# Down blocks of the experts with two neighbouring rows on each partition, and transposes that read every second column

## What is computed

```python
def swiglu(x, w_gate, w_up, w_down):
    return (jax.nn.silu(x @ w_gate) * (x @ w_up)) @ w_down

def moe_swiglu(x, w_router, w_gate, w_up, w_down):
    ...
    for e in range(N_EXPERTS):
        out = out + combine[..., e:e + 1].astype(x.dtype) * swiglu(x, w_gate[e], w_up[e], w_down[e])
    return out
```

## Time and profile before

| | |
|---|---|
| median of 3 runs | 1136.45 us (1135.53 to 1136.66) |
| the profiled execution, its own time | 1137.84 us |
| its span, first to last instruction | 1136.0 us |
| TensorE busy | 1107.8 us (98%), 5842 matmuls |
| VectorE, ScalarE busy | 643.2 us (57%), 467.8 us (41%) |
| moved by DMA | 300.08 MB, mean 264 GB/s |
| chain that ended last | PE 87%, DMA 5%, DVE 3%, ACT 2%, issue 2% |

### The profile page before, as it was taken

One profiled execution on the slowest core, in us unless ns is written; L12 is line 12 of the kernel. 1 busy time (PEld: TensorE's weight loads), 2 busy tenths in 40 slices (PEclk: granted clock), 3 DMA queues, 4 the chain that ended last, 5 costly groups with the idle time before them and its releaser, 6 DMA issues.

```text
span 1136.0 us, 14603 instructions
## 1 busy us (share of the span) xinstructions
PE 1107.8 (98%) x5842; PEld 813.6 (72%) x5842; DVE 643.2 (57%) x745; ACT 467.8 (41%) x598; POOL 43.8 (4%) x45
## 2 busy tenths in 40 slices
PE   7999999999999999999999999999999999999996
PEld 6777878888887788876666666666666666666664
DVE  4877675545467886764655534554553465555235
ACT  4556544443335565143344433333343343443220
POOL 3000020000014000000000000000000000000001
PEclk9999999999999999999999999999999999999998
DMA  9943266555546600089999999899999989999962
GB/s 297 345 147 115 86 196 201 185 185 185 171 163 207 228 1 1 1 295 386 357 367 353 350 353 385 293 394 377 326 388 362 376 295 382 375 350 378 359 270 78
DMA packets 126814, 300.08 MB, mean 264 GB/s; under 512 B 4970, under 2 KB 7160, under 8 KB 126736
## 3 DMA queue, kind: packets, MB, share of 16 engines
q1 hardware_dynamic: 124336, 291.52, 71.2%
q0 software_dynamic: 2112, 6.87, 2.2%
q10 hardware_dynamic: 288, 0.63, 0.2%
HBM read 297.88 MB, written 1.12 MB: 263 GB/s over the span
## 4 chain that ended last, share of the span: by engine, by line
PE 87%; DMA 5%; DVE 3%; ACT 2%; issue 2%; SPq 0%; POOL 0%; POOLq 0%; DVEq 0%; ACTq 0%
PE bank L1599 23%; PE bank L1600 21%; PE bank L1671 12%; PE bank L2064 7%; PE bank L1699 6%; PE bank L2074 4%; PE bank L1789 2%; PE bank L1898 2%; DMA raw<-in_w_in 2%; DMA raw<-in_moe_w_gate 1%; PE bank L1883 1%; PE bank L1815 1%; PE bank L2042 1%; PE bank L1604 1%; DMA raw<-in_moe_w_up 1%
## 5 line engine op out<-in xcount | busy, mean ns | idle before, releaser
L1439 DVE TENSOR_TENSOR w_lo<-raw,w_hi 128x2048 fp32r<-128x2048 f32 x83 | 190.3, 2292 | 271.6 <-ACT w_hi L909 271.6
L1599 PE MATMUL bank<-w_hi,xT_hi 128*128 128x512 f32 (+1 forms) x784 | 312.1, 400 | 0.5 <-ACT w_hi L737 0.5
L1600 PE MATMUL bank<-w_hi,xT_lo 128*128 128x512 f32 (+1 forms) x784 | 302.6, 388 | 0.0
L909 ACT ACTIVATE w_hi<-raw 128x2048 fp32r<-128x2048 f32 x83 | 158.7, 1912 | 240.0 <-PE bank L1671 133.4
L1032 DVE TENSOR_TENSOR w_lo<-raw,w_hi 128x2048 fp32r<-128x2048 f32 x62 | 142.0, 2291 | 103.5 <-ACT w_hi L728 103.0
L1599 PEld LDWEIGHTS bank<-w_hi,xT_hi 128*128 128x128 f32 x784 | 147.9, 189 | 64.4 <-issue 25.6
L1600 PEld LDWEIGHTS bank<-w_hi,xT_lo 128*128 128x128 f32 x784 | 148.1, 189 | 27.2
L1671 PE MATMUL bank<-w_lo,xT_hi 128*128 128x512 f32 (+1 forms) x640 | 167.4, 384 | 0.1
L728 ACT ACTIVATE w_hi<-raw 128x2048 fp32r<-128x2048 f32 x64 | 122.6, 1918 | 97.6 <-PE bank L1671 45.0
L1671 PEld LDWEIGHTS bank<-w_lo,xT_hi 128*128 128x128 f32 x640 | 118.2, 188 | 24.5 <-DVE w_lo L1042 0.5
L1599 PE MATMUL bank<-w_hi,hT_hi 128*128 128x512 f32 x312 | 124.7, 400 | 2.3 <-issue 2.3
(11 more groups left out here) (217 smaller groups left out, 1060.3 us busy)
## 6 DMA issues: line engine op xcount, KB each, us to landing
raw<-in_moe_w_up SPq DMA_DIRECT2D x70, 1024.0 KB, 9.0
raw<-in_moe_w_down SPq DMA_DIRECT2D x70, 1024.0 KB, 8.4
raw<-in_moe_w_gate SPq DMA_DIRECT2D x69, 1024.0 KB, 8.6
raw<-in_w_in SPq DMA_DIRECT2D x23, 1024.0 KB, 8.6
raw<-in_ffn_w_gate SPq DMA_DIRECT2D x11, 1024.0 KB, 5.1
raw<-in_ffn_w_up SPq DMA_DIRECT2D x11, 1024.0 KB, 5.2
raw<-in_ffn_w_down SPq DMA_DIRECT2D x11, 1024.0 KB, 4.9
raw<-in_w_out SPq DMA_DIRECT2D x8, 1024.0 KB, 6.1
```

The lines of the kernel that those rows point to most:

```text
L909: nc.scalar.activation(w_hi[:, m % NH, :], raw[:, n % NR, :], ACT.Copy).then_inc(hi_done, 1)
L1439: nc.vector.tensor_tensor(w_lo[:, m % NH, :], raw[:, (BASE_MOE + load[at[o]]) % NR, :], w_hi[:, m % NH, :].bitcast(F32), ALU.subtract).the ...
L1599: nc.tensor.matmul(o, hi, wh, start=start, stop=False)
L1600: nc.tensor.matmul(o, lo, wh, start=False, stop=False)
```

## The change

A down block puts rows 2p and 2p + 1 on partition p, which are neighbours in memory, 8 KB in all. Part k of the buffer now holds rows 2p + k. For the products to pair the same features, the transposes of the activations take for tile 2i + k not 128 columns in a row but every second of the 256 columns of block i, from column k on. Gate and up blocks, and the dense layer, stay as they are.

```diff
+        def hidden_rows(k, at=0):
+
+            first = at + k // 2 * 2 * P + k % 2
+            return slice(first, first + 2 * P - 1, 2)
+
...
                 if kind == "down":
-                    src = moe_w_down[0, bass.ds(e, 1), c * 256:(c + 1) * 256, :]
+                    src = moe_w_down[0, bass.ds(e, 1), c * 256:(c + 1) * 256, :].rearrange("o (p k) n -> p (o k) n", k=2)
                 else:
                     w = moe_w_gate if kind == "gate" else moe_w_up
                     k = D // 2
                     src = w[0, bass.ds(e, 1), part * k:(part + 1) * k, c * CW:(c + 1) * CW]
-                load(n, src.rearrange("o (k p) n -> p (o k) n", p=P), free, first)
+                    src = src.rearrange("o (k p) n -> p (o k) n", p=P)
+                load(n, src, free, first)
...
                 for k in range(4):
-                    ins = nc.tensor.transpose(bank[:, 4, k * P:(k + 1) * P], hid[:, tt, k * P:(k + 1) * P], ident)
+                    ins = nc.tensor.transpose(bank[:, 4, k * P:(k + 1) * P], hid[:, tt, hidden_rows(k)], ident)
...
                     ins = nc.tensor.transpose(bank[:, 5, k * SMALL:(k + 1) * SMALL],
-                                              hid_s[0:SMALL, c % 2, k * P:(k + 1) * P], ident[0:SMALL, 0:SMALL])
+                                              hid_s[0:SMALL, c % 2, hidden_rows(k)], ident[0:SMALL, 0:SMALL])
```

## The result

The changed kernel took 1142.21 us in the median of 5 runs (1141.12 to 1143.80), the kernel before 1136.45 (1134.61 to 1138.64): the ratio is 1.0057, 95% interval 1.0043 to 1.0071. The medians are 5.8 us apart, two and a half times the 2.3 us that the prediction took as what can be told from no change. The ratio is not the quotient of the two medians: times 1136 us it is 6.5 us, with an interval of 4.9 to 8.1.

The account below looks back on a forecast made before the run. The prediction took TensorE to bound the kernel. From the runs' median of 1136.45 us it took a 0.5 us gain from transfers and price 0 for transposes: 1135.9 us, range 1134.4 to 1140.4.

Parts of the forecast that it names:

- The bound: Expert stage: TensorE bounds it, busy 624.51 of 628 us; DMA has 70 us to spare over the stage.
- The transfers: Down-block loads: 8 KB pieces save 0.075 us a block, 5.3 us of DMA time over 70 blocks.
- What of it reaches the end: TensorE's 1.1 us wait for a gate block at 788.6 us: 0.5 us comes off, bounds 0 and 1.1.
- SyncE's queue: Down-load issue on SyncE: one DMA instruction a block before and after, 373 ns median; piece count hardly shows.
- The transposes: Expert activation transposes on TensorE: stepped weight loads stay at 139 and 137 ns, price taken as 0.
- The other value it had priced: Transposes' loads at the slow kind's pace: 4.3 us for small experts, 0.2 for large, together 4.5 us.
- The rule it leaned on: Transposes' stepped SBUF reads: step two of a 4-byte type has two hits a line, so price 0.
- The weight loads slow down: Rival at the 21 small-expert transpose groups: price 4.5 us, time 1140.4; chance 0.23.
- its far end: Rival for all 196 transposes: loads take twice 139 ns with no cover, 27 us, time 1163; chance 0.03.
- the pieces did not stay at 4 KB: Rival on down loads: the view's loops do not fold, pieces stay 4 KB, time 1136.4; chance 0.07.
- were not slower: Rival on down loads: longer pieces fall back to 2.70 us a block, time 1137.5; chance 0.04.
- lateness did not go for good: Rival on TensorE's waits for landings after 633 us: all 3.4 us removed, time 1133.0; chance 0.07.

Follow-up runs that it names:

- experiment 1: Against the kernel before: transposes step by two columns, down blocks loaded as before (wrong features, only time read); 1141.84 us, ratio 1.0053.
- experiment 2: Against the kernel before: down blocks in 8 KB pieces, transposes read neighbouring columns (wrong features, only time read); 1135.64 us, ratio 1.0002.
- experiment 8: The changed kernel once more, against the kernel before on the same chip; 1140.96 us, ratio 1.0045.
- experiment 5: Against the kernel before: only the 84 small-expert transposes step by two columns, down blocks as before (only time read); 1140.44 us, ratio 1.0040.
- experiment 4: Against the kernel before: 8 KB pieces, ScalarE and VectorE put even and odd columns apart so transposes read neighbours; 1136.77 us, ratio 1.0012.
- experiment 9: 8 KB pieces with columns put apart by ScalarE and VectorE ahead of the transposes, once more, against the kernel before; 1135.76 us, ratio 0.9996.

## Why the prediction was wrong, point by point

The forecast was 1135.9 us, a gain of 0.5; the measured time is 1142.2, above the range, and the direction is the one given 0.23.

- **The bound.** Right, but for one reading: the DMA row has 6 and 2 in its last two slices, not eight or nine in all but the last. TensorE's stream sets the time; experiment 1 puts 6.0 us on it with no change of a transfer, experiment 2 takes 8960 packets away with no change of the time.
- **The transfers.** The mechanism and its size were right: the views fold to pieces of 8 KB, 115376 packets as named, landings 2.45 us apart for 2.475 forecast (2.50 in experiment 2), and 5.7 us less queue time for 5.3. The page's estimate (the Trainium skill, DMA: Bandwidth & Descriptors, "Why small descriptors are slow (HBM only)") of 1.2% for this step was too small beside these 0.08 us of 2.55, some 3%; the trace's own step from 2 KB to 4 KB was the better guide.
- **What of it reaches the end.** The step named one wait of 1.1 us at 788 us and took half of it as the gain. In the first profile of the changed kernel the expert matmuls never wait for a landing. But in the profile of experiment 1, with its old 4 KB pieces, they don't either; in the second profile of the changed kernel (experiment 8) they wait as in the kernel before, and in that of experiment 5, with 4 KB pieces, more. Experiment 8 first, then 5:

```profile
PE bank L2070 <- DMA raw<-in_moe_w_gate: 1.2, 1, 1.2
PE bank L2070 <- DMA raw<-in_moe_w_up: 0.5, 1, 0.5
...
PE bank L2070 <- DMA raw<-in_moe_w_gate: 2.0, 2, 1.6
PE bank L2070 <- DMA raw<-in_moe_w_up: 0.5, 1, 0.5
PE bank L2080 <- DMA raw<-in_moe_w_down: 0.2, 1, 0.2
```

  Such waits come and go between executions of one kernel by a microsecond or two. The one in the profile can't be counted on in another execution, and reading a gain from it was a mistake, though a small one. Experiments 2, 4 and 9 put the pieces at 0.2 us slower, 1.4 us slower and 0.5 us faster, each with 1.2 to 1.4 us on either side, so a gain of 0.5 is neither shown nor excluded.
- **SyncE's queue.** That the count of pieces hardly shows in the instruction's time was read from two and four pieces a partition (373 ns for both). With one it takes 333 ns; nothing hung on it.
- **The transposes.** Here the prediction failed, at "I take 0, the row of the same instruction". A row with neighbouring columns says nothing of a stepped read, so a price of nothing had no row behind it, and the row of the slow kind (191 ns) turned out the nearer one: the stepped load takes 202 to 206. The other value it had priced was good: 0.204 us for a small group, measured 0.23; 4.3 us for the 21 groups, 4.8 by the rows and 4.5 in experiment 5. The large groups were put at 0.2 us and are 1.1 by the rows, where the matmuls now start (0.63 - 0.279) / 3 = 0.117 us apart for 0.109, about the pace of the stepped loads in a small group; in the time it is not to be told from none.
- **The rule it leaned on.** The Trainium skill (SBUF — State Buffer, the note on "cachelines") says that two hits on a line of 16 bytes keep the full rate. The trace disagrees: at two hits the bare transposing loads go from 0.061 us apart to (0.55 - 0.206) / 3 = 0.115, and at one hit they take hardly longer (207 ns for 206). It stood in the prediction as an aside, but beside the unstepped row it is the only thing there that speaks for a price of 0.
- **The rivals.** "The weight loads slow down" is what happened, with its place and size: 1140.4 forecast, 1142.2 and, in the second comparison, 5.1 us over its own runs of before, which is 1141.6 on the first scale. It should have been the forecast: with TensorE busy 624.51 of 628 us and gains priced at 1.1 us, 3.4 at the very end, against losses of 4.5 and up, an unknown on TensorE's own stream weighs more than a saving beside it. The range ended at that rival's bare sum and so took in only half of its spread; 0.03 for its far end did not cover the 1.8 us that were missing. Of these the groups by the rows are 5.9 - 4.5 = 1.4; the rest is of the size of the 0.5 us of gain that was counted in. The others did not occur: the pieces did not stay at 4 KB, were not slower, and lateness did not go for good.

## What to carry to other kernels

Before a layout moves a stride from a DMA to an operand of TensorE, ask which engine the stage is bound by, and who can do the stepping for nothing. Here ScalarE and VectorE read a bank at step two in the same 595 and 684 ns, while a transposing weight load of fp32 went from 137 to 206 ns, with nothing over it in groups whose matmuls are short. And a cheaper transfer is worth only the waits for landings that come back in every execution; compare two or three profiles before pricing one.

## What the hardware showed beyond what was expected

- A transposing weight load of 128 fp32 columns takes 137 to 139 ns with neighbouring columns, 202 to 206 at step two, 204 to 207 at step four, with 32 rows or 128.
- A plain load of the same width, of F32R tiles, takes 188 ns with neighbours and 193 to 194 at step two, and these 5.5 ns do lengthen a stream of matmuls of 512 columns, although each load runs beside one of them.
- SyncE's DMA instruction for a down block takes 333 ns with one piece a partition, 373 with two (whether by the pieces or by the simpler view was not tried apart):

```profile
L539 SPq DMA_DIRECT2D raw<-in_moe_w_down x70: 332/333/1747, 636.5 to 1096.7; - x70
```
